# The first matmuls behind each LayerNorm on the raw residual, with mean and variance applied to their result

## What is computed

```python
def layer_norm(x, g, b):
    mu = mean(x); var = mean(square(x - mu))
    return (x - mu) * rsqrt(var + EPS) * g + b

def swiglu(x, wg, wu, wd):
    return (silu(x @ wg) * (x @ wu)) @ wd

def decoder_layer(x, pos, lp, past):
    x = layer_norm(ALPHA * x + 0.5 * swiglu(x, ...first FFN...), ln_g[0], ln_b[0])
    y, st = token_mixing(x, pos, lp, past)
    x = layer_norm(ALPHA * x + y, ln_g[1], ln_b[1])
    x = layer_norm(ALPHA * x + 0.5 * swiglu(x, ...second FFN...), ln_g[2], ln_b[2])
    return x, st
```

## Time and profile before

| | us |
|---|---|
| median of 3 runs | 1460.26 (1459.71 to 1460.30) |
| the profiled execution, its own time | 1459.3 |
| span of that execution, first to last instruction | 1457.5 |
| PE busy | 1302.7 (89%) |
| DVE busy | 806.6 (55%) |
| ACT busy | 523.8 (36%) |
| POOL busy | 94.5 (6%) |

### The profile page before, as it was taken

One profiled execution on the slowest core, in us unless ns is written; L12 is line 12 of the kernel. 1 busy time (PEld: TensorE's weight loads), 2 busy tenths in 40 slices (PEclk: granted clock), 3 DMA queues, 4 the chain that ended last, 5 costly groups with the idle time before them and its releaser, 6 DMA issues.

```text
span 1457.5 us, 24721 instructions
## 1 busy us (share of the span) xinstructions
PE 1302.7 (89%) x9806; PEld 1146.9 (79%) x9806; DVE 806.6 (55%) x1531; ACT 523.8 (36%) x768; POOL 94.5 (6%) x160
## 2 busy tenths in 40 slices
PE   6999997997777989999799999799877787999994
PEld 5999996564455789999799999775545566999993
DVE  5555547765565265554565553678464644555433
ACT  3433435222343153433354333433133434343331
POOL 9000001001000010000200000100100001000001
PEclk9999998998889989999989999899987898999997
DMA  7654573756072225545635555576522522554540
GB/s 255 207 191 144 159 227 128 243 180 211 10 215 67 79 98 190 192 139 160 213 120 174 173 159 178 187 229 203 178 94 89 144 77 96 174 173 155 160 120 30
DMA packets 254823, 226.70 MB, mean 156 GB/s; under 512 B 12628, under 2 KB 234946, under 8 KB 254594
## 3 DMA queue, kind: packets, MB, share of 16 engines
q1 hardware_dynamic: 250530, 220.79, 47.6%
q0 software_dynamic: 4192, 4.53, 0.9%
HBM read 221.42 MB, written 3.86 MB: 155 GB/s over the span
## 4 chain that ended last, share of the span: by engine, by line
PE 80%; DVE 11%; issue 3%; SPq 2%; ACT 2%; DMA 1%; POOL 0%; DVEq 0%; ACTq 0%
PE bank L717 21%; PE bank L718 20%; PE bank L719 20%; PE bank L639 7%; PE bank L880 3%; PE bank L942 1%; PE bank L726 1%; PE bank L727 1%; SPq L405 1%; DVE bc_pages L1846 1%; PE bank L992 1%; DVE bc_pages L1863 1%; DVE rstd L1746 1%; SPq L414 1%; DVE w_low L1447 1%
## 5 line engine op out<-in xcount | busy, mean ns | idle before, releaser
L717 PE MATMUL bank<-x_high,w_low 128*128 128x264 f32 x1408 | 408.0, 290 | 26.7 <-DVE x_low L1429 22.6
L718 PE MATMUL bank<-x_low,w_high 128*128 128x264 f32 x1408 | 404.7, 287 | 0.0
L719 PE MATMUL bank<-x_high,w_high 128*128 128x264 f32 x1408 | 404.2, 287 | 0.0
L1447 DVE TENSOR_TENSOR w_low<-weights,w_high 128x2048 fp32r<-128x2048 f32 (+1 forms) x172 | 347.8, 2039 | 69.7 <-ACT w_high L1161 53.8
L717 PEld LDWEIGHTS bank<-x_high,w_low 128*128 128x128 f32 x1408 | 270.4, 192 | 30.9 <-issue 27.9
L718 PEld LDWEIGHTS bank<-x_low,w_high 128*128 128x128 f32 x1408 | 271.5, 193 | 0.0
L719 PEld LDWEIGHTS bank<-x_high,w_high 128*128 128x128 f32 x1408 | 269.9, 192 | 0.0
L717 PE MATMUL bank<-hidden_high,w_low 128*128 128x264 f32 x704 | 204.9, 291 | 0.0
L719 PE MATMUL bank<-hidden_high,w_high 128*128 128x264 f32 x704 | 200.0, 284 | 0.0
L718 PE MATMUL bank<-hidden_low,w_high 128*128 128x264 f32 x704 | 199.6, 284 | 0.0
L1203 ACT ACTIVATE w_high<-weights 128x2048 fp32r<-128x2048 f32 (+1 forms) x88 | 163.8, 1861 | 6.3 <-DMA weights<-in_ffn_wu_dram 6.1
(11 more groups left out here) (311 smaller groups left out, 1694.5 us busy)
## 6 DMA issues: line engine op xcount, KB each, us to landing
weights<-in_ffn_wg_dram SPq DMA_DIRECT2D x44, 1024.0 KB, 5.2
weights<-in_ffn_wu_dram SPq DMA_DIRECT2D x44, 1024.0 KB, 7.5
weights<-in_ffn_wd_dram SPq DMA_DIRECT2D x64, 704.0 KB, 5.9
weights<-in_w_in_dram SPq DMA_DIRECT2D x20, 1024.0 KB, 5.9
bc_pages<-in_cache_bc_kv_dram SPq DMA_DIRECT2D x128, 128.0 KB, 2.3
ring<-in_cache_bs_kv_dram SPq DMA_DIRECT2D x96, 128.0 KB, 2.1
ring<-in_cache_bw_kv_dram SPq DMA_DIRECT2D x12, 512.0 KB, 4.0
weights<-in_cache_bs_kv_dram SPq DMA_DIRECT2D x32, 128.0 KB, 2.4
```

Source lines behind the costliest of these rows:

```text
L717: mm(out, w_low, v_high, start=start, stop=False)
L718: mm(out, w_high, v_low, start=False, stop=False)
L719: return mm(out, w_high, v_high, start=False, stop=stop)
L1447: tt(low(k, half), raw(k, half), high(k, half).bitcast(F32), ALU.subtract).then_inc(low_done, 1)
```

## The change

A product with the normed x is linear in the residual: with W and one token, W(g (z - mean) r + b) = r (W(g z) - mean W g) + W b, where r is the reciprocal of the deviation. So at norms 0 to 4 the first matmul group runs on raw chunks g z (raw_high, raw_low), each made as soon as its z is there, and on two more columns, -g and b (266 columns in all). DVE later corrects each bank: copy of the two columns, multiply-add with the mean, product with r (`rescaled`); the last addition goes into ScalarE's bias or the next DVE operation. The normed x is still made, for all other groups.

On the queues: PE runs the group chunk by chunk over four banks, and the last chunk's statistics behind the raw chunk 1. In an FFN, group 1 goes chunk by chunk too, into banks 4 to 7, and group 2 waits until group 0's banks are read. Splits of the weight block behind the raw one move into the norm, one half before the reciprocal, one behind it; ScalarE's warm Silu moves ahead of the normed x. DVE makes raw_low of a chunk ahead of the next z. raw_low overlays x and raw_high the place of x_low, so ScalarE's write of x waits until PE has used the raw chunk. In the mix no fold stands in the first group and two behind each tile of g = 1; DVE's first two page products move ahead of the last z of the FFN before; two caches and the w_in blocks' high parts change places in the ring, and SP waits once more, ahead of cache 1.

```diff
+                        if m == 6:
+                            sp.wait_ge(*used(l, WIN_USE))
...
+                def opening(g):
+
+                    k = base + g
+                    pe.wait_ge(low_done, halves_before(l, k) + 2)
+                    halves = [[w(k, i).rearrange("p (c f) -> p c f", c=KC) for w in (high, low)] for i in range(2)]
+                    n = 3 * l + 2 * j - 1
+                    if g:
+                        pe.wait_ge(var_done, n + 1)
+                    for c in range(KC):
+                        if g:
+                            pe.wait_ge(low_x_ready, (n + 1) * KC + c + 1)
+                            x_parts, cols = (x_high[:, c, :], x_low[:, c, :]), TOK
+                        else:
+                            pe.wait_ge(raw_low_done, n * KC + c + 1)
+                            x_parts, cols = (raw_high[:, c, :], raw_low[:, c, :]), TOK + 2
+                        for q in range(2):
+                            for i, full in enumerate((gate_full, up_full)):
+                                wh, wl = (w[:, c, q * P:(q + 1) * P] for w in halves[i])
+                                last = product(banks[4 * g + 2 * q + i][:, 0:cols], wh, wl, *x_parts, c == 0, c == KC - 1)
+                                if c == KC - 1:
+                                    last.then_inc(full, 1)
+                        if g == 0 and c < KC - 1:
+                            last.then_inc(raw_used, 1)
+                        if g == 0 and c == 1:
+                            stats(n, KC - 1)
+
...
+                        if f and isinstance(n0, int) and n0 == 4:
+
+                            pe.wait_ge(hidden_done, f * FC + q + 1)
...
                 for g in range(SLOTS):
-                    group(base + g, halves_before(l, base + g), 2 * g)
+                    if f and g < 2:
+                        opening(g)
+                    else:
+                        group(base + g, halves_before(l, base + g), 2 * g)
...
                 for g in range(KC):
                     if g >= 2:
                         pe.wait_ge(z_done, n * KC + g - 1)
                     y_chunk(g, banks[4 + g % 2][:, 0:TOK]).then_inc(y_full, 1)
                     if g:
-                        stats(g - 1)
-                stats(KC - 1)
+                        stats(n, g - 1)
+                if not split_x(n):
+                    stats(n, KC - 1)
...
                 k = WIN_USE
-                for m in range(4):
-                    out = bank_v() if m < 2 else bank_a()
-                    for c in range(KC):
-                        if m == 0:
-                            pe.wait_ge(low_x_ready, (3 * l + 1) * KC + c + 1)
-                        last = product(out[:, 0:TOK], *parts_of(k, c, slice(m * P, (m + 1) * P)),
-                                       mix_x_high[:, c, :], mix_x_low[:, c, :], c == 0, c == KC - 1)
-                    last.then_inc(v_full if m < 2 else a_full, 1)
-                    if m:
-                        compress()
+                n = 3 * l
+                opened = [banks[4], banks[5], bank_a(), bank_a()]
+                for c in range(KC):
+                    pe.wait_ge(raw_low_done, n * KC + c + 1)
+                    for m in range(4):
+                        if c + m == 1:
+                            pe.wait_ge(z_done, (n + 1) * KC)
+                        last = product(opened[m][:, 0:TOK + 2], *parts_of(k, c, slice(m * P, (m + 1) * P)),
+                                       raw_high[:, c, :], raw_low[:, c, :], c == 0, c == KC - 1)
+                        if c == KC - 1:
+                            last.then_inc(conv_full if m < 2 else a_full, 1)
+                    if c < KC - 1:
+                        last.then_inc(raw_used, 1)
+                    if c == 1:
+                        stats(n, KC - 1)
 
                 for g in range(4):
                     k = WIN_USE + 1 + g
@@ -776,10 +832,14 @@
                         r, col, _ = rows_of(t)
                         out = bank_v()
                         for c in range(KC):
+                            if g + t == 0:
+                                pe.wait_ge(low_x_ready, (n + 1) * KC + c + 1)
                             last = product(out[0:r, :], mix_x_high[:, c, col], mix_x_low[:, c, col],
                                            *parts_of(k, c, slice(0, 512)), c == 0, c == KC - 1)
                         last.then_inc(v_full, 1)
                         compress()
+                        if g == 1:
+                            compress()
                         if g >= 2:
...
                     go(ln_squares[:, g % 2, :], z[:, g, :], ACT.Square).then_inc(sq_done, 1)
+                    if split_x(n):
+                        go(raw_high[:, g, 0:TOK], z[:, g, :], ACT.Copy, scale=params[:, n // 3, n % 3 * 8 + g:n % 3 * 8 + g + 1])\
+                            .then_inc(raw_high_done, 1)
                 norm(n)
 
             def norm(n):
                 l, i = n // 3, n % 3
+                if split_x(n):
+                    ahead_l, ahead_k = next_use(n)
+                    split_high(ahead_k, landed_value(ahead_l, ahead_k), (0,))
                 act.wait_ge(var_done, n + 1)
                 go(rstd[:, 0, :], rstd[:, 0, :], ACT.Sqrt).then_inc(std_done, 1)
+                if split_x(n):
+                    if i:
+
+                        go(warm[:, :], warm[:, :], ACT.Silu)
+                    split_high(ahead_k, landed_value(ahead_l, ahead_k), (1,))
                 for c in range(KC):
                     act.wait_ge(norm_done, n * KC + c + 1)
                     affine = dict(bias=params[:, l, 24 + i * 8 + c:25 + i * 8 + c],
                                   scale=params[:, l, i * 8 + c:i * 8 + c + 1])
+                    if split_x(n):
+                        act.wait_ge(*raw_free(n, c))
                     go(x[:, c, :], z[:, c, :], ACT.Identity, **affine).then_inc(x_ready, 1)
                     if split_x(n):
                         go((x_high if i else mix_x_high)[:, c, :], z[:, c, :], ACT.Identity, **affine).then_inc(high_x_ready, 1)
-                if i != 0 and n < 3 * DEPTH - 1:
-
-                    go(warm[:, :], warm[:, :], ACT.Silu)
 
...
+
+                def opening():
+
+                    split_high(base + 2, landed_value(l, base + 2), (0,))
+                    for q in range(2):
+                        act.wait_ge(scaled, 2 * (3 * l + 2 * j - 1) + q + 1)
+                        go(silu[:, q, :], silu[:, q, :], ACT.Silu, bias=tails[:, 2 * q, 1:2]).then_inc(silu_done, 1)
+                    split_high(base + 2, landed_value(l, base + 2), (1,))
+                    for q in range(2):
+                        n = f * FC + 2 + q
+                        act.wait_ge(gate_full, n + 1)
+                        act.wait_ge(hidden_ready, n - 1)
+                        go(silu[:, q, :], banks[4 + 2 * q][:, 0:TOK], ACT.Silu).then_inc(silu_done, 1)
...
-                split_w_in(1)
                 for c in range(2):
-                    ps = bank_a()
-                    go(gelu[:, c, :], ps[:, 0:TOK], ACT.Gelu_apprx_tanh).then_inc(a_free, 1)
+                    made.next(a_full)
+                    act.wait_ge(scaled, 6 * l + c + 1)
+                    go(gelu[:, c, :], gelu[:, c, :], ACT.Gelu_apprx_tanh, bias=tails[:, 2 + c, 1:2]).then_inc(gelu_done, 1)
...
+            def raw_low_of(n, c):
+
+                at_ = n % 3 * 8 + c
+                dve.wait_ge(raw_high_done, n * KC + c + 1)
+                stt(raw_low[:, c, 0:TOK], z[:, c, :], params[:, n // 3, at_:at_ + 1], raw_high[:, c, 0:TOK].bitcast(F32),
+                    ALU.mult, ALU.subtract).then_inc(raw_low_done, 1)
+
+            def rescaled(dst, ps, tail, done=None):
+
+                step(copy(tail, ps[:, TOK:TOK + 2]))
+                read = stt(dst, mean_sb[:, :], tail[:, 0:1], ps[:, 0:TOK], ALU.mult, ALU.add)
+                step(read)
+                if done is not None:
+                    dve.sem_inc(done, 1)
+                return tt(dst, dst, rstd[:, 0, :], ALU.mult)
+
             def residual(n, factor, ahead):
 
+                if split_x(n):
+                    tail_columns(n)
                 for g in range(KC):
                     ahead(g)
+                    if g and split_x(n):
+                        raw_low_of(n, g - 1)
                     dve.wait_ge(y_full, n * KC + g + 1)
                     stt(z[:, g, :], banks[4 + g % 2][:, 0:TOK], factor, x[:, g, :], ALU.mult, ALU.add).then_inc(z_done, 1)
+                if split_x(n):
+                    raw_low_of(n, KC - 1)
                 dve.wait_ge(stat_done, (n + 1) * KC)
                 copy(mean_sb[:, :], banks[6][:, 0:TOK]).then_inc(mean_done, 1)
                 dve.wait_ge(mean_done, n + 1)
@@ -1487,8 +1602,12 @@
                 step(tt(rstd[:, 1, :], mean_sb[:, :], mean_sb[:, :], ALU.mult))
                 step(tt(v, banks[7][:, 0:TOK], rstd[:, 1, :], ALU.subtract))
```

(58 more changed lines are left out.)

88 lines of the change are left out of this document (56 added, 32 removed).

## The result

The changed kernel took 1482.6 us (median of 4 runs, 1478.5 to 1484.6) beside 1460.28 of the kernel before: a ratio of 1.0156, with a 95% interval of 1.0137 to 1.0175. It is 22 us slower. The forecast was 1452, 8 us faster, and the range ended at 1465. The profiled execution took 1478.5, with a span of 1476.7, 19.2 more than before.

A forecast was written before the change was run, and what follows sets the result against it. PE ends nearly everything, so its idle time, chiefly waits for x_low, can be won. 1459.3 - 19.2 (three FFN norms) + 11.0 (two mixes) = 1451.1, on the median 1452.0 us; range 1436 to 1465.

The forecast's parts named there:

- The FFN norms: Three norms before an FFN: PE's hole falls from 7.5 to 3.9 us, gaining 6.4 us each, 19.2 in all.
- The 2.6 us wait inside group 2: FFN norms: PE waits 2.6 us for DVE's second half split, which also covers 2 us of slow clock.
- The rival that the splits share a rate with GpSimd and run 2.3 times slower: Five norms: splits cost 2.1 us more each, nothing is left of the gain, 1462.6 us; chance 0.14.
- The mix as far as the LRU matmuls: Layer 0 mix: raw opening leads by some 9 us, DVE loses most; LRU matmuls start at 263.6 against 267.4.
- The lead there: Mix at the LRU matmuls: 3.8 us ahead of before, less up to 2.4 at the low clock.
- The mix behind it: Mix up to cache 3: lead becomes lag; 5.0 us late, up to 7.4; 5.5 lost at each of two, 11.0.
- Page 9: SP's queue in the mix: released one tile later because fold 7 follows the third tile; 292.6 against 284.0, 8.6 late.
- The half of w_in: Mix, fourth w_in block: second half issued at 275.2 instead of 258.15, landing 5.1 later, its split done at 284.5.
- now vanish: SP from page 9 to cache 3, 52 us nearly without a break: 3.6 us of waits for folds disappear.
- group 1 goes at SP's pace: Mix rival: SP needs 33 us for six pages against PE's 19, costing 13 each mix, 1467.1 us; chance 0.15.
- the two columns: FFN raw group: the two extra columns of 266 cost under 0.1 us.

The follow-up runs named there:

- ffn_fill: Raw opening at the three FFN norms alone, mix as in the kernel before, plus 22 unused matmuls in PE's hole behind each raw group; 1449.8 us, ratio 0.9919.
- ffn_only: Raw opening at the three FFN norms alone; mix, page folds, SP's order and x_low's rows as in the kernel before; 1444.15 us, ratio 0.9873.
- base_2: Kernel before with x_low moved by 2 elements, its rows still 264 apart; 1460.4 us, one time.
- before_266: Kernel before with x_low's rows 266 elements apart instead of 264; 1462.0 us, ratio 1.0020.
- before_272: Kernel before with x_low's rows 272 elements apart instead of 264; 1461.0 us, one time.
- before_280: Kernel before with x_low's rows 280 elements apart instead of 264; 1458.5 us, one time.
- xlow_264: Changed kernel with x_low given its own layout again, rows 264 elements apart, over the raw part with rows 266 apart; 1476.3 us, ratio 1.0088.
- rope_first: Changed kernel, x_low rows 264 apart, folds of pages 0 and 1 behind raw group, fourth w_in block before page 2, first token tile before corrections; 1449.8 us.

## Why the prediction was wrong, point by point

**The FFN norms: right.** Third norm, us after the second-last statistics:

| | forecast | measured |
|---|---|---|
| raw group ends | 13.4 | 13.9 |
| both half splits beside GpSimd | 5.3 | 5.29 |
| first normed matmul | 17.3 | 16.75 |
| group 1 ends | 28.9 | 31.6 (28.9 with the hole filled) |
| last half split of w_low ends | 34.7 | 34.4 |
| group 2 ends | 43.4 | 43.7 |

The 2.6 us wait inside group 2 did not appear at this norm, as PE came 2.7 late from the slow clock; at the other two it was 1.25 us. The prediction had said that the one lies in the other, and ffn_fill shows it with a wait of 2.2. The gain is 6.1 to 6.2 at each norm in ffn_only, 18.4 in all, and 19.2 was forecast. The rival that the splits share a rate with GpSimd and run 2.3 times slower fell: 2.84 and 2.45 us.

That GpSimd's eight subtractions grew by 4.0 us, all of it in the two pieces beside a split, while the splits lost 0.2 to 0.6, is one engine standing while the other runs. It is what the Trainium skill, SBUF — State Buffer, section "SBUF: two separate sides", says of VectorE with two SBUF inputs and a GpSimd instruction that reads SBUF: whichever starts first holds the pair of ports for its whole instruction. The trace agrees with it.

**The mix as far as the LRU matmuls: nearly right.** Taking off the 1.77 us of the first FFN: first token tile starts 237.9 (forecast 238.5), ends 245.3 (245.0), VectorE's first token tile ends 257.4 (257.3), LRU matmuls 265.0 (263.6). The lead there is 2.3, not 3.8; the third tile ran at the low clock behind its 5.3 us wait, as the text had allowed.

**The mix behind it: the step that failed.** The forecast was 5.0 late at cache 3, and it measured 14.8. Two terms are wrong.
- Page 9 was to be 8.6 us late and is 12.4. The half of w_in was issued 1.0 later than forecast and landed 6.7 us after its issue instead of 5.1, and its issue alone took 1.75 us; its split ended 2.65 late. The rest, 1.2, is the tile behind the 6.64 us wait at the low clock (a fold took 1.08 instead of 0.64).
- From page 9 to cache 3 the forecast took 3.6 us off, because SP's waits for folds "now vanish". They did not: SP still waited 4.6 us, in one wait, and the stretch grew from 55.8 to 58.1. PE, late, waited 3.03 us for page 12, ran slow behind it, and folded page 13 10.0 us after page 12 (337.31 - 327.33) where a tile and its fold take 6.3. SP, which waited for that fold, issued page 15 only at 338.72. SP and PE wait for each other by turns there: a delay of one is no slack of the other, and each turn adds a hole and a slow tile.

So 3.8 and 5.9 us of each mix were mis-sized in the same direction, on a mechanism that was named. The rival "group 1 goes at SP's pace" had it at 13 a mix; it was 15 by cache 3 and 16 by the next norm. Its number came nearest, its mechanism only in part: SP was not held by its own pace there but stood idle 8.0 us before page 4 and 5.0 before page 5 (from its timeline), for folds. I gave it less weight because SP can load a page ahead of PE. The text had the order that speaks against that: page m is loaded only after fold m-2, so with no fold in the raw group SP has nothing to load ahead.

**Not in the prediction: x_low's rows.** The diff gives x_low two columns more in each row, and I priced the two columns and not the layout. It costs 0.17 us a group and 6 us in all. Without it the changed kernel would still be slower (1476.3).

The sum from measured terms: 1459.3 - 18.4 + 32.1 + 6 = 1479.0; the profiled run took 1478.5. The 32.1 and most of the 6 are read from that same profile, so this shows that no term is missing and is no second proof.

## What to carry to other kernels

A step that is moved takes its releases with it: before laying an opening differently, list every transfer that waits on the moved work, and follow the queue behind that transfer to the point where an engine needs its end. Where two engines release each other by turns, do not credit the waits of one as slack for the other; price the turn. And try a change by its places: here three of five were worth 18.4 us, and two cost 32 in the order they were given.

## What the runs showed of the hardware

- The pace of matmuls at the full clock depended on the layout of one moving operand, from 11.53 us (rows 280 apart) over 11.60 (264) to 11.76 (266, changed kernel) for 96 of them; in base_2, before_266, before_272 and before_280 only x_low's layout was changed, and with it the place of what lies behind x_low in the ring. Which property of the addresses decides was not found.
- The same wait of PE was not always followed by a lower clock. Behind the 2.89 us hole of an FFN norm the lower level lasted 6.8 us (changed kernel, third norm), 3.4 us (its second and fifth) or did not come at all (xlow_264, second norm). What decides between them was not tried.
- The part of the mix behind PE's first use of cache 3 took from 164.1 to 172.2 us in the runs above, where the instructions are the same. In the two that I compared, before and rope_first, PE's listed waits there add up to 36.8 and 36.5 us. The granted clock differs there. Windows of 29 us from PE's first use of cache 3, before and then in rope_first (columns as in the earlier trace rows, PE alone):

```profile
341.00:370.00 29.00, 24.14 (x182) 0.76 0.54 175
```

```profile
342.00:371.00 29.00, 24.15 (x143) 0.62 0.54 175
```

PE is busy for the same share and has a clock of 0.62 instead of 0.76. The 7.7 us of rope_first's first mix over before arise behind cache 3 but for 1.2, and its wide range (1442.0 to 1453.5) fits that. What picks the one or the other was not tried.
